# Sample attention in eighteen steps of four groups instead of twenty-four steps of one batch

## The reference

```python
# branch 0, stick-breaking
z = einsum('bqhd,bkhd->bhqk', q, k) * scale
log_keep = where(mask, log_sigmoid(-z), 0.0)
suffix = cumsum(log_keep, axis=3, reverse=True) - log_keep
a = where(mask, exp(log_sigmoid(z) + suffix), 0.0)
# branch 1, forgetting: s = scores + g_k - g_q, masked softmax
# branch 2, sparse: softmax over the keys that the indexer chose
isc = einsum('bqhk,bqh->bqk', relu(isc), wib)
vals, idx = lax.top_k(isc, topk)        # topk = 132 of 528 keys
# every branch
out = einsum('bhqk,bkhd->bqhd', p, v)
```

## Time and profile before

| | us |
|---|---|
| median of 3 runs | 2502.47 (2501.01 to 2503.35) |
| profiled execution | 2501.38 |
| its span, first to last instruction | 2499.6 |
| TensorE busy | 2409.5 (96%) |
| VectorE busy | 1262.9 (51%) |
| ScalarE busy | 576.5 (23%) |
| DMA, mean over the span | 156 GB/s |
| sample attention, layer 0 / layer 1 | 168.36 / 168.14 |

### The profile page before, as it was taken

The page is one execution under the profiler, slowest core; times in us unless marked ns, Lnnn a source line. Parts: engine busy times, 40 slices in busy tenths (PEclk is TensorE's granted clock), DMA queues, the critical chain, the costliest instruction groups (busy, mean ns, idle before and its releaser), DMA issues.

```text
span 2499.6 us, 41793 instructions
## 1 busy us (share of the span) xinstructions
PE 2409.5 (96%) x17156; PEld 2070.0 (83%) x17156; DVE 1262.9 (51%) x2728; ACT 576.5 (23%) x1316; POOL 62.9 (3%) x100
## 2 busy tenths in 40 slices
PE   7999999999999899999999999999999989999998
PEld 6999996875666589999989999878656655999998
DVE  3566422624577435565255663325175864266642
ACT  3000022124534322001130000311345441310011
POOL 0000000000012100000000000000000120000000
PEclk8999999999999899999999999999999998999999
DMA  8354243861369542442425533367424793323332
GB/s 313 110 189 166 96 156 103 261 219 64 121 204 319 168 150 102 169 153 98 138 102 181 190 115 116 133 177 251 145 81 152 251 302 129 135 68 128 100 114 72
DMA packets 299564, 389.96 MB, mean 156 GB/s; under 512 B 33677, under 2 KB 245385, under 8 KB 299378
## 3 DMA queue, kind: packets, MB, share of 16 engines
q1 hardware_dynamic: 281538, 339.52, 40.5%
q0 software_dynamic: 10752, 38.93, 4.8%
q10 hardware_dynamic: 7088, 8.87, 1.0%
HBM read 377.66 MB, written 9.62 MB: 155 GB/s over the span
## 4 chain that ended last, share of the span: by engine, by line
PE 87%; DMA 4%; DVE 3%; ACT 3%; SPq 2%; issue 1%; ACTq 0%; DVEq 0%
PE PS L702 28%; PE PS L749 12%; PE PS L955 9%; PE PS L1149 4%; PE PS L903 4%; PE PS L849 3%; PE PS L685 3%; PE PS L629 3%; PE PS L669 2%; PE PS L797 2%; PE PS L805 2%; PE PS L925 2%; PE PS L1171 2%; PE PS L1163 2%; PE PS L1108 2%; DMA QR<-scr_mask_sample 1%
## 5 line engine op out<-in xcount | busy, mean ns | idle before, releaser
L955 PE MATMUL PS<-H,RING 128*128 128x384 f32 x672 | 225.1, 489 | 0.5 <-DMA RING<-w_in 0.4
L702 PE MATMUL PS<-OT,RING 128*128 128x192 f32 x1216 | 222.5, 326 | 0.0
L702 PE MATMUL PS<-H,RING 128*128 128x192 f32 x1216 | 211.7, 327 | 0.0
L702 PE MATMUL PS<-OT,QR 128*128 128x192 f32 x1216 | 210.0, 326 | 0.0
L702 PEld LDWEIGHTS PS<-OT,RING 128*128 128x128 f32 x1216 | 201.8, 190 | 0.0
L702 PEld LDWEIGHTS PS<-H,RING 128*128 128x128 f32 x1216 | 198.0, 190 | 3.5 <-issue 3.2
L702 PEld LDWEIGHTS PS<-OT,QR 128*128 128x128 f32 x1216 | 199.7, 190 | 0.0
L955 PEld LDWEIGHTS PS<-H,RING 128*128 128x128 f32 x672 | 124.6, 190 | 84.6 <-issue 4.7
L1277 ACT ACTIVATE QR<-QR 128x384 f32<-128x384 f32 x76 | 39.7, 523 | 509.1 <-DVE QR L1793 509.1
L702 PE MATMUL PS<-H,QR 128*128 128x192 f32 x608 | 111.2, 326 | 0.0
L702 PEld LDWEIGHTS PS<-H,QR 128*128 128x128 f32 x608 | 100.9, 190 | 0.0
(11 more groups left out here) (305 smaller groups left out, 4173.0 us busy)
## 6 DMA issues: line engine op xcount, KB each, us to landing
RING<-ffn_w_in SPq DMA_DIRECT2D x80, 1024.0 KB, 7.2
RING<-w_in SPq DMA_DIRECT2D x64, 768.0 KB, 6.2
QR<-w_ada SPq DMA_DIRECT2D x34, 1024.0 KB, 10.0
BIG<-w_ada SPq DMA_DIRECT2D x34, 1024.0 KB, 10.7
RING<-ffn_w_out SPq DMA_DIRECT2D x32, 768.0 KB, 4.7
RING<-ffn_w_out SPq DMA_DIRECT2D x32, 640.0 KB, 5.4
QKT<-cache_sb_k SPq DMA_DIRECT2D x16, 768.0 KB, 5.6
QR<-cache_sb_v POOLq DMA_DIRECT2D x16, 768.0 KB, 5.0
```

The source lines that it names most:

```text
L702: mm = pe.matmul(PS[:, bank, GROUP[g]], a[:, k, :], x[:, k, :], start=(k == 0), stop=(k == 3))
L955: mm = pe.matmul(PS[:, bank, 0:T], w[:, k, (n % 3) * P:(n % 3 + 1) * P], H[:, k, :], start=(k == 0), stop=(k == KD - 1))
```

## The change

A step now takes four groups, whichever batch they belong to: 24 groups of a branch are six units, and three branches make 18 steps. The fourth strip of 32 partitions, empty before, is used. A unit spans two batches.

- TensorE: the keys of a unit are turned in two pieces, three groups early in the step (`turn_three`) and the fourth at its end (`turn_fourth`), into bank 0 again (bank 3 for units 0 and 1). The probabilities of the 16 new keys are turned on their own (`turn_new_probs`), into bank 7, and wait for `o_free`. The scores read `QBLK` itself and no copy of it.
- Gate tiles: one stands ahead of step 0 (`GATE_FIRST_UNIT`), six in steps 1, 3, 5, 8, 12 and 16.
- Top-k rounds are dealt out anew (`ROUND_S`), and the last now stands in step 9 of 18, not 12 of 24.
- SyncE: a key buffer is loaded when the unit with its batch's last group has been turned; the bias rows come in eight DMAs of 16 rows; the mask is stored at step 10 and waited for at once.
- POOL: four value buffers instead of two.
- Memory: score, bias and probability buffers move onto the masks, the prompt mask's bias and the norm's scratch; the masks are loaded anew for layer 1.

```diff
-GATE_STEP = dict(zip((0, 1, 2, 3, 4, 6, 15), range(17, 24)))
+GATE_FIRST_UNIT = 17
+GATE_UNIT = dict(zip((1, 3, 5, 8, 12, 16), range(18, 24)))
-ROUND_S = {0: 2, 1: 2, 2: 2, 3: 2, 4: 2, 6: 2, 8: 1, 9: 1, 10: 1, 11: 1, 12: 1}
+ROUND_S = {0: 1, 1: 3, 3: 3, 5: 3, 6: 1, 7: 1, 8: 4, 9: 1}
...
-NSTEP = NB * NBR
+UNIT = 4
+NU = NB * NPAIR // UNIT
+NSTEP = NU * NBR
+NCACHE = NB * NBR
+KBUF, VBUF = 3, 4
+def unit_groups(s):
+    return [(s // NU * NB + g // NPAIR, g % NPAIR) for g in range(s % NU * UNIT, s % NU * UNIT + UNIT)]
+def last_unit(n):
+    return divmod(NPAIR * n + NPAIR - 1, UNIT)
...
 SyncE
-                for s in range(NSTEP):
-                    if s == 2 * NB:
-                        sp.wait_ge(msk_stored, l * 16 + 16)
-                    load_bias(s)
-                    if s + 3 < NSTEP:
-                        load_keys(s + 3)
-                    if s == 5:
-                        gates(7)
-                    if s == max(ROUND_S) + 2:
-                        sp.wait_ge(msk_ready, l * 3 + 3)
-                        sp.dma_start(m_s, WKS).then_inc(msk_stored, 16)
+                for s in range(-2, NSTEP):
+                    for n in range(KBUF, NCACHE):
+                        if last_unit(n - KBUF)[0] == s + 2:
+                            load_keys(n)
+                    if s == 3:
+                        gates(7)
+                    if s == max(ROUND_S) + 1:
+                        sp.wait_ge(msk_ready, l * 3 + 3)
+                        sp.dma_start(m_s, WKS).then_inc(msk_stored, 16)
+                        sp.wait_ge(msk_stored, l * 16 + 16)
+                    if NU <= s + 2 < NSTEP:
+                        load_bias(s + 2)
...
 load_keys
+                    if n >= KBUF:
+                        u, i = last_unit(n - KBUF)
+                        sp.wait_ge(kt_ready, 2 * (l * NSTEP + u) + 1 + i // 3)
...
 TensorE
+                def turn_new_probs(s):
+                    pe.wait_ge(o_free, l * NSTEP + s + 1)
+                    pe.transpose(PS[0:NT, 7, 2 * P:3 * P], ES[s % 2][:, PAST:KEYS], IDENT[:, :]).then_inc(st_ready, 1)
...
                     if s + 2 < NSTEP:
-                        turn(s + 2)
-                    if s in GATE_STEP:
-                        gate_tile(GATE_STEP[s], 3, GATE_STEP[s])
+                        turn_three(s + 2)
+                    if s >= 1:
+                        turn_new_probs(s - 1)
+                    if s in GATE_UNIT:
+                        gate_tile(GATE_UNIT[s], 3, GATE_UNIT[s])
                     if s >= 1:
                         values(s - 1)
+                    if s + 2 < NSTEP:
+                        turn_fourth(s + 2)
...
 VectorE
+                    for i, j, b, a in unit_spans(s):
+                        g = 3 * (s // NU) + a
+                        o = OT[:, g:g + j - i, b * NT + NPROMPT:(b + 1) * NT + NPROMPT]
+                        V.tensor_copy(o[0:64], src[0:64, i:j, 0:NT])
+                        ins = V.tensor_copy(o[64:128], src[64:128, i:j, NT:2 * NT])
...
 POOL
-                    pool.wait_ge(pv_ready, l * NSTEP + s + 1)
+                    if n >= VBUF:
+                        pool.wait_ge(pv_ready, l * NSTEP + last_unit(n - VBUF)[0] + 3)
```

271 lines of the change are left out of this document (148 added, 123 removed).

## The result

The changed kernel takes 2530.3 us (median of 4 runs, 2527.98 to 2530.91) against 2502.68 us for the kernel before beside it (2501.01 to 2503.35): a ratio of 1.0108, 95% interval 1.0095 to 1.0121, 27.6 us slower. The forecast was 2501 (2478 to 2524). The profiled execution took 2530.91 us, its span 2529.1.

The account below looks back on a forecast made before the run. TensorE's work and waits were taken as the bound, with the bias loop and DMA engines near; 147.4 us plus 20.3 of late things gave a 167.7 us stage against 168.4, so 2501 us in all (2494 to 2508; wide range 2478 to 2524).

Parts of the forecast that it names:

- the late biases: Bias rows behind a late key load at steps 8, 11 and 14: 2.5 us late each, 7.5 in all.
- the overpriced mask: Sample mask stored in step 10, its landing awaited at once: step 12 gets its rows 6.0 us late.
- stage without late loads: Head, first step, gate steps, other steps and tail of one sample attention stage: 147.4 us, plus 0.7 for top-k rounds.
- rival 3: Four strips do not run beside each other in values: 16.2 us on the forecast, 2517; chance 0.05.
- The pair without a gate: Ordinary pair of steps 13 to 15, with no gate tile between: bias late by 0.8 us.
- the keys (0.8): Key loads behind a late turn: 8.3 us to land where about 8 are to spare, 0.8 us (0 to 2).
- The eighth starts 3.1 later: SyncE's bias loop: eighth issue 3.1 us after the first, landing 6.06 (4.62 at best) later, late by 2.7 (1.3 at best).
- rival 2: Slower through SyncE's queue at step 12: late things 31.8 us, stage 179.2, whole 2524, halfway 2513; chance 0.29.
- A wait of some 6 us for the mask should do the same: TensorE's clock falls after the mask wait, with a gate tile behind it: 2.5 us (0 to 4).
- No gate tile covers these: Late biases stay uncovered: the new 0.11 us transposition waits for o_free ahead of the gate tile, which queues behind it.
- rival 1: Late loads mostly short: late things 8.3 us, stage 155.7, whole 2476, or 2488 with half that gain; chance 0.32.
- The signs that I had named: Forecast wrong if step 12's wait is under 3 or over 9 us, or steps between gates under 5.3 or over 6.2.

Follow-up runs that it names:

- e8: Changed kernel without the value loads of 20 of the 24 caches of a layer, the first four read over and over: 2479.8 us, ratio 0.9903.
- e14: Changed kernel with POOL issuing a value load only when the bias under way has landed: 2501.7 us, ratio 0.9990.
- e2: Changed kernel with one bias DMA of 128 rows per step (two in mixed steps) in place of eight of 16: 2539.6 us, ratio 1.0150.
- e17: Changed kernel plus 32 unneeded transpositions on TensorE ahead of each late wait (steps 6, 8, 11, 12, 14): 2518.5 us, ratio 1.0057.
- e9: Changed kernel with TensorE's 16-row transposition, which waits for o_free, moved behind the gate tile: 2543.0 us, ratio 1.0158.
- e12: Changed kernel with mask stored early and waited for late, bias before keys, and gate tiles in steps 1, 4, 7, 9, 12, 14: 2523.2 us, ratio 1.0075.
- e11: Changed kernel with mask stored early and waited for late, bias before keys, value loads held until the bias landed: 2492.4 us, ratio 0.9956.
- e7: Kernel before the change with one bias DMA of 96 rows per step in place of six of 16 rows: 2515.6 us, ratio 1.0053.
- e4: Changed kernel with the mask stored after step 8 and its landing waited for only before the bias of step 12: 2519.8 us, ratio 1.0066.

## Why the prediction was wrong

Two steps of the working failed. The slower records of TensorE behind a wait were priced at one wait only, 2.5 us for 12.4 measured; and the late biases, with the gate weights, were put at 9.5 us of waits for 16.1 measured, which the overpriced mask and the small terms hid in the sum. The terms of the forecast stand beside what the changed kernel and the one without bias show, for layer 0:

| part | forecast | measured |
|---|---|---|
| stage without late loads | 147.4 + 0.7 = 148.1 | 150.2 |
| waits (bias, mask, weights, keys) | 17.1 | 18.9 |
| clock | 2.5 | 12.4 |
| stage | 167.7 | 181.4 |

- *Steps without late loads*: right. Values in four strips cost 1.43 us, rival 3 did not happen. Gate steps are 0.3 longer than forecast and the others 0 to 0.3, apart from the two waits for keys of 0.8 and 1.0 us; head 8.8 (9.0 forecast), first step 6.4 (6.6), tail 12.9 (13.9).
- *The sum of the waits*: right within 2 us, by luck: errors cancel. I took 2.5 for each late bias and 2.0 for step 6; TensorE's idle time grew by 4.2, 4.6 and 4.0 us, and by 3.4. The mask, taken at 6.0, showed as 3.8. Its rows were even later than forecast, 25.2 us after the scores of step 10 (22.5 to 24), with 11.5 us for the store's landing (10 forecast, and 10.0 in the kernel before); but step 11 had already lost 6.4 us, and step 12 began that much later. The pair without a gate (0.8) showed nothing at steps 13 to 15, and the keys (0.8) nothing beyond what the kernel without bias has.
- *Landing*: here the working of the waits failed. "The eighth starts 3.1 later, and lands 6.06 (4.62 at best) after that" took 6.06 from the third branch of before as the upper value. It was 8.1 and 8.2 at steps 6 and 8, in the second branch. The medians for the forgetting bias went from 4.2 to 6.6 us, for its keys from 5.9 to 8.8, for the weights from 8.1 to 14.5; the mask rows stayed at 4.4 to 4.5, and the third branch's keys fell from 8.3 to 5.6. And the argument against rival 2, that the stage's mean stays near 261 GB/s, was no argument: the mean fell to 241 while the landings of the second branch grew by half and more. That the value loads beside them did it is shown by e8 and e14. That it is the bursts, with idle engines between, is seen around step 13 and not tested by itself.
- *Issue time*: the rows for it were right in most steps (3.6 to 4.3 us for eight; 9.9 at step 6), its use was not. Against the Trainium skill (DMA: Bandwidth & Descriptors, "Issuing engines are not separate DMA queues"), by whose words the time to initiate a DMA is usually small, I let the issues set the loop. e2 cut them to 0.6 us and lost 9 us, because one large DMA landed later. That does not show the issues to be free. It shows that they were not the term to gain on in this way. The same section's point, that the issuing engines are not separate DMA queues, is what e8 shows in numbers: POOL's loads slowed SyncE's.
- *Clock*: the term that failed the sum. "A wait of some 6 us for the mask should do the same, with a gate tile behind it: 2.5 us (0 to 4)". It did the same at the mask, where the records behind it took the 2.5 us forecast, and at four more places with waits of TensorE of 2.5 to 4.7 us, for which I had forecast waits but no clock: 9.8 us more, 12.4 in the stage. e17 shows that at least part of this is time on the path, by bringing 12 us of the whole back, 5.6 in this stage, without shortening VectorE's waits in sum. The rule that I cited (the Trainium skill, Perfetto Trace Analysis, "Matmul Optimizations": the matmul engine scales its power with use) pointed there, and the trace agrees; I used it to price one rival, where it belonged in every wait.
- *"No gate tile covers these"*: true of the order of the instructions, but no loss. e9 put the cover there and lost 13 us.
- *Rival 2* came nearest, 2524 against 2530, with 31.1 us of late things (its 31.8 without the 0.7 of top-k rounds) against 31.2 measured. That is mostly luck: it had 9 us at the mask for 3.8, 8.1 for the three biases for 12.7, and 5 us of clock for 12.4. Its mechanism, "through SyncE's queue at step 12", is only part of it. By e8 the order of SyncE costs 5.6 and 9.4 us in the two stages once no values load beside it.
- Two small slips changed nothing. A stage of 167.7 us is 0.7 under layer 0 but only 0.4 under layer 1, so the two layers give 1.1 and not 1.4. And rival 1's "fewer bytes per microsecond" had no row: the bytes stayed (43.70 MB for 43.71).
- The signs that I had named did not catch the error. The wait at step 12 lay between 3 and 9 us and the steps between gates in 5.3 to 6.2, and the forecast was wrong all the same, since none of the signs looked at the clock outside step 12.

What stays open: whether it is that two value loads are released at once, or that they are four deep, that makes the same bytes worse than before. No run here has other buffer counts. Nor is it excluded that steps without a tile simply ask for more than the DMA engines move: e12, which was meant to test this, failed by its top-k rounds. Against it, the kernel without bias moved 374 and 376 GB/s in steps 11 and 14 and waited for nothing there; for it, e11 still takes 14 us more than that kernel in the stage.

## What to carry to other kernels

When a chain already has waits of a few microseconds, price each one twice, the wait and the slower records of TensorE behind it: here 19 us of waits came with 12 us of slower records. Ask of every small load on the path what large loads another queue will release at the same moment, and try holding those back until it has landed, watching that they do not come late themselves; a mean transfer rate says nothing about that. When an instruction is moved behind a long one, count what is queued behind its consumer as well.

## What the runs showed of the hardware

- One or two broadcast DMAs of 66 to 264 KB land much later than the last of six or eight of 33 KB with the same rows: 8.4 to 16.8 us in the chain of e2 and 8.9 to 11.0 in that of e7 (layer 0), against 4.3 to 8.2 (once, in e4, 12.3). Counted from the first issue there is little between them in three of four steps, and 4.9 us in the fourth. Cutting the number of issues made both kernels slower, by 9 and 12 us.
- Eight issues of 33 KB took SyncE 3.6 to 4.3 us in most steps, and 9.9 us at step 6, right behind loads of 1.57 MB of weights and two of keys, with the DMA engines' share at 1.04.
- Adding 160 useless transpositions a stage made the kernel 12 us faster (e17).
- The same store of 264 KB to memory landed in 2.3 us (e4), 5.2 (e8) and 11.5 us (the changed kernel). Beside it the DMA engines moved 114 to 212 GB/s, 48 to 268, and 304 to 348 in its first 7 us.
- The length of TensorE's wait alone did not decide on the clock: 2.44 us ahead of the scores of step 1 left them at 1.10 us in layer 0, and the same 2.44 us made them 1.99 us in layer 1 (the changed kernel and the one without bias alike). In e17 a wait of 3.34 us at step 12, behind 32 transpositions, left the gate tile at 5.33 us.
- Making value loads wait for the landed bias made the kernel 28.6 us faster (e14), with no byte and no instruction of the computation changed, although TensorE then waited up to 6.48 us for values.
